# The sparse block's h2 in PSUM, z in two banks instead of four, and 52 of the u blocks split by GpSimd beside pairs of VectorE dot products

## What is computed

```python
qry = (xb @ w_q).reshape(TB, PEER_HEADS, PEER_D_KEY)
v1, i1 = lax.top_k(s1, K)          # s1, s2: scores against 128 + 128 keys
v2, i2 = lax.top_k(s2, K)
...
sc, ci = lax.top_k(cand, K)        # 16 of the 256 pairs, for each of 8 heads
gate = jax.nn.softmax(sc.astype(jnp.float32), axis=-1)
act = jax.nn.gelu(jnp.einsum('thed,td->the', u_table[idx], xb).astype(jnp.float32), approximate=False)
return jnp.einsum('the,thed->td', (gate * act).astype(xb.dtype), v_table[idx])
```

## Time and profile before

| | before |
|---|---|
| median of 3 runs | 1565.91 us (1565.29 to 1567.02) |
| profiled execution, its own time | 1564.76 us |
| its span, first to last instruction | 1563.0 us |
| PE busy | 1515.3 us (97%) |
| DVE busy | 1223.1 us (78%) |
| ACT busy | 561.5 us (36%) |
| POOL busy | 547.2 us (35%) |

### The profile page before, as it was taken

How to read it: one execution, slowest core, us unless ns; L and a number is a source line. 1 busy time by engine, 2 the same in 40 slices (tenths; PEclk the granted TensorE clock), 3 DMA queues, 4 the chain that set the end, 5 groups by cost and what they waited for, 6 DMA issues and landing times.

```text
span 1563.0 us, 22972 instructions
## 1 busy us (share of the span) xinstructions
PE 1515.3 (97%) x8069; PEld 1353.2 (87%) x8069; DVE 1223.1 (78%) x2336; ACT 561.5 (36%) x816; POOL 547.2 (35%) x297
## 2 busy tenths in 40 slices
PE   6999989999989999999999999979999999999999
PEld 6879658788989999999999999968888888888887
DVE  4537473288989999989999999648878788787886
ACT  4363442222423333334444444333232332322321
POOL 2213241232643222752333323314434434344341
PEclk9999979999999999999999999999999999999999
DMA  5400202221467877997798898999999999999993
GB/s 198 142 28 1 108 1 67 87 75 68 162 226 266 276 260 258 367 413 289 296 324 311 284 332 309 356 327 373 354 350 355 352 356 354 351 359 349 354 355 125
DMA packets 181667, 399.37 MB, mean 256 GB/s; under 512 B 12260, under 2 KB 111844, under 8 KB 180072
## 3 DMA queue, kind: packets, MB, share of 16 engines
q1 hardware_dynamic: 144744, 264.41, 48.3%
q0 software_dynamic: 36864, 134.23, 23.3%
HBM read 346.16 MB, written 52.43 MB: 255 GB/s over the span
## 4 chain that ended last, share of the span: by engine, by line
PE 83%; DVE 8%; POOL 3%; DMA 3%; issue 1%; ACT 1%; SPq 0%; DVEq 0%; ACTq 0%
PE banks L1820 25%; PE banks L1613 15%; PE banks L1884 11%; PE banks L1886 11%; PE banks L1885 11%; PE banks L1855 5%; POOL u_rows L669 3%; DMA u_rows<-in_u,idx 1%; DMA v_raw<-in_v 1%; PE banks L1801 1%; PE banks L1664 1%; DVE wo_lo L1241 1%; PE banks L1723 1%; DVE picked L1385 1%; PE banks L1748 1%
## 5 line engine op out<-in xcount | busy, mean ns | idle before, releaser
L669 POOL DMA_INDIRECT u_rows<-in_u,idx x128 | 202.9, 1585 | 362.8 <-DVE z L1423 336.7
L691 POOL DMA_INDIRECT v_rows<-in_v,idx x128 | 205.5, 1606 | 333.4 <-DVE x_res L1550 294.8
L1884 PE MATMUL banks<-v_hi,w_hi 128*128 128x512 f32 x768 | 299.6, 390 | 7.4 <-DVE v_lo L1497 7.4
L1886 PE MATMUL banks<-v_hi,w_lo 128*128 128x512 f32 x768 | 299.3, 390 | 0.0
L1885 PE MATMUL banks<-v_lo,w_hi 128*128 128x512 f32 x768 | 299.3, 390 | 0.0
L1497 DVE TENSOR_TENSOR v_lo<-v_raw,v_hi 128x1024 fp32r<-128x1024 f32 x128 | 153.6, 1221 | 120.4 <-ACT v_hi L982 120.4
L982 ACT ACTIVATE v_hi<-v_raw 128x1024 fp32r<-128x1024 f32 x128 | 125.8, 1049 | 339.0 <-PE banks L1886 320.2
L1820 PE MATMUL banks<-h_lo,u_hi 128*128 128x384 f32 x1024 | 209.9, 338 | 0.0
L1820 PE MATMUL banks<-h_hi,u_lo 128*128 128x384 f32 x1024 | 199.2, 335 | 9.5 <-DVE u_lo L1412 9.5
L1820 PE MATMUL banks<-h_hi,u_hi 128*128 128x384 f32 x1024 | 203.6, 340 | 0.3 <-ACT u_hi L909 0.3
L1820 PEld LDWEIGHTS banks<-h_hi,u_lo 128*128 128x128 f32 x1024 | 179.4, 188 | 11.1 <-DVE u_lo L1412 11.1
(11 more groups left out here) (256 smaller groups left out, 1926.2 us busy)
## 6 DMA issues: line engine op xcount, KB each, us to landing
u_raw<-in_uT SPq DMA_DIRECT2D x128, 512.0 KB
v_raw<-in_v SPq DMA_DIRECT2D x128, 512.0 KB, 5.9
act_scratch<-act_out SPq DMA_DIRECT2D x128, 192.0 KB
act_in<-act_scratch SPq DMA_DIRECT2D x32, 768.0 KB, 8.4
gates<-gate_scratch SPq DMA_DIRECT2D x32, 768.0 KB, 12.4
gate_scratch<-stage SPq DMA_DIRECT2D x11, 2048.0 KB, 8.1
wi_raw<-in_w_in SPq DMA_DIRECT2D x8, 1024.0 KB, 8.7
wq_raw<-in_w_q SPq DMA_DIRECT2D x8, 1024.0 KB, 5.6
```

Source lines behind the costliest of these rows:

```text
L669: nc.gpsimd.indirect_dma_start(u_rows[U_SLOT[s]][:], None, a["u"], bass.IndirectOffsetOnAxis(ap=idx0[:, s:s + 1], axis=0)).then_inc(ug_in[ ...
L691: nc.gpsimd.indirect_dma_start(v_rows[s % V_ROWS][:], None, v_flat, bass.IndirectOffsetOnAxis(ap=idx0[:, s:s + 1], axis=0)).then_inc(vg_in ...
L1884: mm(y, w, v_hi[q][:, j, ds], start=first and j == 0, stop=False)
L1886: end = mm(y, w_lo[q][:, j, t * P:(t + 1) * P], v_hi[q][:, j, ds], start=False, stop=last and j == GROUP - 1)
```

## The change

Four things are changed together, and all of them lie in the PEER part.

1. h2 of the sparse block is copied once by ScalarE from SBUF to PSUM banks 2 and 3 (`h2_first`), and all 128 dots read it there. The first dot waits for the copy.
2. z has two banks (`Z_BANKS`), 0 and 1, so block n waits for the GELU of block n-2 in place of n-4.
3. GpSimd splits, besides blocks 0 to 11, the 52 even blocks 16 to 118 (`SHARED`). VectorE opens each of these turns with a memset of one column, whose semaphore GpSimd's split waits for, and then issues two dots. The gathers stand between these splits in GpSimd's queue.
4. VectorE's order is new: dots stand in pairs in the even turns from turn 14 on, single ones in some odd turns (`DOTS_AT`); pieces of `choose` are issued until they add up to 2150 for each turn (`PIECE_SIZE`). The number of dots is the same in each stretch: 66, 54 and 8.

```diff
-POOL_SPLITS = 12
+POOL_FIRST, SHARE_FROM = 12, 16
+Z_BANKS = 2
...
-DOTS_PRE = 66
-DOTS_MAIN = [1, 1, 1, 1, 1, 1, 1, 2]
-DOTS_POST = [2] * 4
...
-DOT_SIZE, SLOT_SIZE = 1170, 2800
+SHARED = list(range(SHARE_FROM, POST, 2))
+DOTS_AT = [2 if n + 2 in SHARED else 0 for n in range(POST)] + [2] * 4 + [0] * 4
+for _n in [*range(PRE - 17, PRE, 2)][:8] + [*range(PRE + 5, POST, 6)]:
+    DOTS_AT[_n] += 1
...
+PIECE_SIZE = 2150
...
-            for s in range(SLOTS):
+            s = 0
+            for n in range(len(DOTS_AT)):
+                while s < SLOTS and (U_BEFORE[s] is None or U_BEFORE[s] < sum(DOTS_AT[:n])):
+                    gather_u(s)
+                    s += 1
+                if n + 2 in SHARED:
+
+                    pool.wait_ge(share_open, SHARED.index(n + 2) + 1)
+                    split_u(n + 2)
...
+            for j in (2, 3):
+                emptied(act, JOBS[(len(JOBS) - 1) // 8 * 8 + j][0])
+            nc.scalar.activation(h2_first, h2_nat[:, 0, :], ACT.Copy).then_inc(h2_placed, 1)
...
-                nc.scalar.activation(act_out[:, j % RING, :], ps[:, j % RING, 0:ND], ACT.Gelu).then_inc(act_ready, 1)
+                nc.scalar.activation(act_out[:, j % RING, :], ps[:, j % Z_BANKS, 0:ND], ACT.Gelu).then_inc(act_ready, 1)
...
-                nc.vector.tensor_tensor_reduce(rows[:], rows[:], h2_nat[:, 0, :], 1.0, 0.0, ALU.mult, ALU.add,
+                nc.vector.tensor_tensor_reduce(rows[:], rows[:], h2_first, 1.0, 0.0, ALU.mult, ALU.add,
...
-            work, done = rest(), 0
-            for n in range(POOL_SPLITS - 2, PRE):
-                split_u(n + 2)
-                while done < (n - POOL_SPLITS + 3) * SLOT_SIZE:
-                    done += next(work, SLOT_SIZE)
+            def splits_and_dots(n):
+
+                if n + 2 in SHARED:
+                    nc.vector.memset(opened[:, SHARED.index(n + 2):SHARED.index(n + 2) + 1], 0.0).then_inc(share_open, 1)
+                else:
+                    split_u(n + 2)
+                for _ in range(DOTS_AT[n]):
+                    dot()
+
+            work, done = itertools.chain(*(choose(t) for t in range(1, TB))), 0
+            sizes = itertools.cycle(CHOOSE_SIZES)
+            for n in range(POOL_FIRST - 2, PRE):
+                splits_and_dots(n)
+                while done < (n - POOL_FIRST + 3) * PIECE_SIZE:
+                    done += next(sizes)
+                    next(work, None)
...
-                    pe.wait_ge(act_ready, n - (RING - 1))
-                o, q = ps[:, j % RING, 0:ND], j % ring
+                    pe.wait_ge(act_ready, n - (Z_BANKS - 1))
+                o, q = ps[:, j % Z_BANKS, 0:ND], j % ring
```

More of the change, by code:

```diff
@@ L281, in build @@
         tab = at("tab", 186, [P, 3, ND])
+        opened = at("opened", 103.25, [P, len(SHARED)])
         idx0 = at("idx0", 20, [P, SLOTS], I32)
@@ L504, in pre @@
                         save_act(n - 2, j + 2)
-            for i in range(POOL_SPLITS // PRE_BODY):
-                pre(i, True)
-            with sp.Fori(POOL_SPLITS // PRE_BODY, PRE_TRIPS) as i:
+            for i in range(SHARE_FROM // PRE_BODY):
+                pre(i)
+            with sp.Fori(SHARE_FROM // PRE_BODY, PRE_TRIPS) as i:
                 pre(i)
@@ L671, in gather_u @@
                     bass.IndirectOffsetOnAxis(ap=idx0[:, s:s + 1], axis=0)).then_inc(ug_in[U_SLOT[s]], 16)
-            for n in range(POOL_SPLITS):
+            for n in range(POOL_FIRST):
                 split_u(n)
             pool.wait_ge(idx_ready, 1)
-            for s in range(SLOTS):
+            s = 0
[6 more added lines that the diff above has]
+                    split_u(n + 2)
+            while s < SLOTS:
                 gather_u(s)
+                s += 1
             v_flat = a["v"].rearrange("n p d -> (n p) d")
@@ L1439, in _ @@
                 pass
[L1440 to L1448, removed]
-                            yield DOT_SIZE
-                while dots[0] < DOTS_PRE:
-                    dot()
-                    yield DOT_SIZE
-            work, done = rest(), 0
-            for n in range(POOL_SPLITS - 2, PRE):
-                split_u(n + 2)
-                while done < (n - POOL_SPLITS + 3) * SLOT_SIZE:
-                    done += next(work, SLOT_SIZE)
+            def splits_and_dots(n):
+                if n + 2 in SHARED:
+                    nc.vector.memset(opened[:, SHARED.index(n + 2):SHARED.index(n + 2) + 1], 0.0).then_inc(share_open, 1)
+                else:
+                    split_u(n + 2)
+                for _ in range(DOTS_AT[n]):
+                    dot()
+            work, done = itertools.chain(*(choose(t) for t in range(1, TB))), 0
[5 more added lines that the diff above has]
+                    next(work, None)
                 if n == NORM_AT:
@@ L1465, in _ @@
                                                    ps[:, 4 + t, 0:3 * P].rearrange("p (w t) -> p w t", w=3)))
-            for _ in work:
-                pass
+            assert next(work, 0) == 0
             settle()
@@ L1490, in _ @@
                             one_hots(i * MAIN_BATCHES + 2 * j + 2 + n)
-                    for _ in range(DOTS_MAIN[j]):
-                        dot()
             def split_v(g, q, j):
@@ L1516, in post_dots @@
             def post_dots(n):
-                for _ in range(DOTS_POST[n - POST]):
+                for _ in range(DOTS_AT[n]):
                     dot()
```

58 lines of the change are left out of this document (36 added, 22 removed).

## The result

| | before | after |
|---|---|---|
| median of 5 runs, same chip | 1565.62 us (1565.23 to 1567.02) | 1557.91 us (1555.78 to 1558.66) |
| profiled execution, its own time | 1564.76 us | 1557.91 us |
| span | 1563.0 us | 1556.1 us |

The change makes the kernel faster by half a per cent: the ratio is 0.9948, interval 0.9934 to 0.9961, and the medians are 7.7 us apart. The forecast was 6.0 less, 1559.9, with a range from 1557.8. So the sum lacked something on the fast side, and the question is what.

A forecast was written before the change was run, and what follows sets the result against it. TensorE, busy for 1515.3 of 1563.0 us, was taken to bound the kernel. Savings of 5.5 at blocks 12 to 15 and 0.5 at the main stretch gave 6.0 off 1565.91, 1559.9 us; range 1557.8 to 1564.0.

The forecast's parts named there:

- blocks 12 to 15: First stretch, just after choose(0): moving the first dot behind the splits of blocks 12 to 15 saves 5.5 us.
- from there to the first tail block: Start of the main stretch: TensorE's wait for the gate rows goes, 0.5 us less.
- the part of 6.5 without waits: Blocks 12 to 15: without waits block 15 would start at 458.3 in place of 464.83, 6.5 us earlier.
- the 1.0 taken away for a wait ahead of the third part of block 14: Block 14: VectorE's split comes late, a wait of 0.4 to 1.9 us replacing 0.86; taken as 1.0.
- the 1 us that I named as wrong: Tail, left alone by the change: a move of more than 1 us would show the prediction wrong.
- the gathers in the same queue: GpSimd's queue: gathers delay a split by 1 or 2 us, holding up VectorE by at most 2.1; priced at nothing.
- Rival 1: Turns 18 to 24: late GpSimd splits collide with `picked`, TensorE waits for `u_lo`; 1561.4 to 1563.5 us, chance 0.18.
- rival 2: Late loads of u or two z banks stop TensorE, two waits of 1 to 3 us; 1562 to 1566, chance 0.08.
- rival 3: Dots hold up GpSimd's splits wherever h2 lies, in both stretches; 48 us slower, 1614; chance 0.07 in full or part.
- such an offset (1.15): Whole kernel: the profiled execution took 1564.76 us, 1.15 less than the median of 1565.91; the 6.0 came off the median.
- the better case: No gaps at the split of 14 and no small losses, 1558.9 us, or a better tail, to 1557; chance 0.07.
- VectorE's load (3.92 against 3.94 a turn): First stretch: VectorE's work a turn, 3.92 us after against 3.94 before, keeps ahead of TensorE's 4.15; taken as nothing.

The follow-up runs named there:

- The run with VectorE held late: The changed kernel with a useless sum of about 3.5 us on VectorE behind the split of block 12; executed once, profiled at 1564.66 us.
- the kernel with the order alone: The kernel before with no dot before turn 14 of VectorE, all else as it was; 1563.64 us, ratio 0.9983.
- the kernel before with the hold: The kernel before, with GpSimd's gathers of v from the third on waiting until 8 blocks of v are split; 1560.42 us, ratio 0.9960.
- the nine profiles named above: Profiled executions of kernels without held v gathers, leaving out the one with dots from SBUF; their second product took 534.9 to 536.6 us.
- The second comparison: The changed kernel, unaltered, run again on another chip against the kernel before there; 1557.15 us, ratio 0.9940.

## Where the prediction was right, and the step that failed

The sum, by its own steps, between the two profiled executions:

| step | forecast | measured | from |
|---|---|---|---|
| ahead of block 12's third part | 0 | -0.32 | 448.50, 448.82 |
| blocks 12 to 15 | 5.5 | 6.44 | above |
| from there to the first tail block | 0.5 | 0.82 | 989.14 - 464.83 less 982.20 - 458.71 |
| tail | 0 | 0.86 | 1027.61 - 989.14 less 1019.81 - 982.20 |
| second product | 0 | -0.90 | 1563.0 - 1027.61 less 1556.1 - 1019.81 |
| sum | 6.0 | 6.90 | spans 1563.0, 1556.1 |

- **The place was right.** The wait ahead of 13 is gone, and the part of 6.5 without waits measured 6.44.
- **The step that failed is the 1.0 taken away for a wait ahead of the third part of block 14.** The text put it at 0.4 to 1.9 us; it measured nothing, so the place gave 6.44 and not 5.5. The term rests on VectorE's gaps, of which I wrote that they "stood beside the first eight gathers, and will again". They did not. The pieces ran 4 us earlier, at 452 to 456, and took 3.89; the text had 4.3 for them even without gaps, since it took off the 1.5 of the row and not the whole 1.87 of standstill. With that the wait goes at its lower end too, by 0.1 to 0.2 us.
- **Why the gaps stayed away is open in part.** The run with VectorE held late brought gaps and wait back, and in the kernel with the order alone the standstill hit other pieces at the same time, 459 to 461. So the moment matters, and not which piece it is. But the moment does not decide alone: in the changed kernel index pieces (L1401, 459.2 to 460.7) run without a gap, at a DMA share of 1.00 too. What stalls VectorE is not shown.
- **The main stretch** gave 0.82, not 0.5, and all of it lies at the gate rows: from the first part of block 15 to the start of the group of four matmuls ahead of the first gate product it is 239.53 us before and 239.52 after, from there to the next block 5.29 (704.36 to 709.65) and 4.48 (698.23 to 702.71), and to the tail 279.49 in both. A wait of 0.52 costs 0.81, the rest being the stop and the start around it.
- **The tail, priced at nothing, moved by 0.86**, near the 1 us that I named as wrong: waits of 1.6 and 0.3 us went, and 1.0 of these 1.9 was lost again in slower matmuls behind the wait of 2.3 that stayed (2.84 at 1008.35, where a group has 1.66; the granted clock is 0.57 from 1008 to 1012). Before, behind the same 2.33 us of wait at 1015.30, the clock stayed at 1.00.
- **The second product then gave 0.90 back** in these two executions. This is no effect of the change: in the second profile of the same changed kernel that part took 534.9 us (1554.8 - 1019.88), against 536.3 here and 535.4 before. The rows show the clock at work. The stretch 1040 to 1060 with the long wait for `v_lo`, of before, of the changed kernel, of its second profile and of the kernel before with the hold:

```profile
1040.00:1060.00 20.00, 12.58 (x50) 9.96 (x49) 14.07 (x13) 10.16 (x9) 3.35 (x2) 0.83 1.06 366
...
1040.00:1060.00 20.00, 16.69 (x61) 13.55 (x62) 18.71 (x15) 5.86 (x6) 7.94 (x5) 0.76 1.05 377
...
1040.00:1060.00 20.00, 16.61 (x67) 13.71 (x68) 18.80 (x15) 5.93 (x6) 7.78 (x5) 0.84 1.05 377
...
1040.00:1060.00 20.00, 19.49 (x86) 15.81 (x86) 15.20 (x13) 9.13 (x8) 10.66 (x7) 1.00 1.03 366
```

  The changed kernel works on at the lower level for some 6 us behind the wait, to 1049.4, its second profile for some 3, to 1046.4: 61 matmuls against 67 in the same busy time. In the nine profiles named above under the hold on the kernel before, the part took 534.9 to 535.5 us where the clock rose again 3 to 4 us behind the wait, and 536.1 to 536.6 where it did so after 4.6 to 6. The sum had no term for this. So that the sum of the trace (6.90) comes near the forecast is in part luck: -0.32 and -0.90 stand against 0.82 and 0.86.
- **What the change adds was nothing, as priced**: two banks (0.9991 to 1.0009 alone), the dot from PSUM (1213 ns), GpSimd's splits beside dots (2.40), the copy, the gathers in the same queue (two collisions with `picked`, 0.9 and 1.0 us, no wait). Rival 1 and rival 2 did not come; rival 3 is real, but only with h2 in SBUF.
- **The rest of the gap to 7.7** is 0.9, the difference of the medians less that of the profiled executions (7.71 less 6.85). The kernel before was profiled in an execution 0.9 under its median of 1565.62, and 1.4 to 2.0 under its medians on the three later chips. The text noticed such an offset (1.15) and went on as if it could only be the same after. The second comparison gave 9.65, the first 7.7. A part of such differences goes with the clock: of 27 executions of the kernel before on one chip the three with a mean grant of 0.986 took 1567.4 to 1569.2, the one with 0.991 took 1562.5. That the clock is the cause of the rest is not shown. The lower edge, 1557.8, held the better case but no such spread of about 1 us; it should have been near 1556.
- **My reason for the order was half of the truth.** The prediction ascribes 5.5 us to the first dot's place. The order alone gains 6.30 there, but has only 3.53 of it at the first gate product and 2.7 in the end: VectorE's turns stay full, and each delay of it, the 1.88 us standstill first, comes through to TensorE. With the new order but without the sharing 5.9 us of waits come back after block 16. The text counted VectorE's load (3.92 against 3.94 a turn) as a cost to be hidden; what the sharing takes off VectorE is needed to keep the gain. How much of the 7.7 belongs to it alone cannot be said, since the order alone and the change differ in the sizes of the pieces as well.

## What to carry to other kernels

Here a stall behind an instruction that waits for data was cured by order, but the gain was kept only where the engine had slack behind it; read the engine's load in the stretch behind such a place before the gain is booked. VectorE and GpSimd could share this work once the instruction beside the other had one SBUF operand, by a one-time copy to PSUM; the trial with the operand in SBUF costs one edit. Where a wait names an engine, follow its own wait one step further: the 7 us at the second product were a load behind gathers that nobody needed yet, and holding these back gave 6.4 us alone, two thirds of what the change gave on the same chip (9.65). And price a wait with what comes behind it: the stop and start around it, and a clock that may have fallen.

## What the runs showed of the hardware that I had not expected

- A gather's issue on GpSimd waits for a VectorE instruction with two SBUF operands as a split does (3.95 and 4.03 us beside `picked`, 0.94 alone, and 0.94 at 475.29 beside a sum over `picked`, which reads one operand for 3.47 us). With the same order of work the mean over the 128 gathers of u is 1565 ns when the dots read SBUF and 1271 when they read PSUM, so the dots from SBUF held up many of them.
- The dot is no slower from PSUM: 1213 against 1221 ns, and 1.14 against 1.15 us from the start of one to the next instruction. The Trainium skill's page VectorE: DVE Perf Modes (section on the TRN2 errata) gives a PSUM source 62 cycles more, an estimate of 65 ns by its clock. This was not there in 128 dots; the measurement decides.
- Of two dots in a row beside a split, the first runs through and the second stands until the split is done (1.22 and 3.36 us): the two engines take turns by whole instructions. The page SBUF — State Buffer of the Trainium skill (Who interferes with whom) exempts a VectorE instruction with at most one SBUF input; the pair of runs, 1557 against 1601 us, agrees.
- TensorE's clock fell behind some long waits, and the lost clock is part of what the moved dot gave back. Two windows around the wait ahead of block 13, of before and then of the changed kernel:

```profile
452.00:456.00 4.00, 0.94 (x6) 0.62 (x4) 2.00 (x3) 1.06 (x1) 3.09 (x4) 1.00 1.03 409
456.00:460.00 4.00, 3.57 (x13) 3.58 (x14) 3.11 (x28) 0.49 (x1) 2.86 (x4) 0.66 1.00 378
```

```profile
452.00:456.00 4.00, 4.00 (x25) 4.00 (x24) 3.96 (x42) 1.55 (x2) 3.08 (x4) 1.00 0.97 349
456.00:460.00 4.00, 4.00 (x25) 3.90 (x24) 3.97 (x20) 0.94 (x1) 3.39 (x3) 1.00 1.00 401
```

TensorE, having worked 0.94 of the 4 us, then had a mean grant of 0.66: the lower level of 1.2 GHz for some two thirds of the stretch, and 13 matmuls where the changed kernel, busy throughout at 2.4 GHz, made 25. A part of the 13 is the wait itself, up to 456.43. But what the changed kernel is spared here it loses in its tail, behind the wait ahead of 1008.35.
